# A two-block transformer on one core: first attention beside the later input projections and a split output projection

## What is computed

```
xn   = rmsnorm(x, g)
qa, ka, va, qb, kb, vb, f = split(xn @ w_in)          # widths 512,128,128,512,512,512,8
qa, ka, qb, kb            = rmsnorm per head of 64
out_a = softmax(qa ka' / 8 + alibi, window 128, one sink logit per head) va   # 8 heads, 2 kv heads
c     = cumsum(log_sigmoid(f + b))
out_b = softmax(qb kb' / 8 + c[t] - c[s], causal) vb                          # 8 heads
x = x + concat(out_a, out_b) @ w_out                  # 1024 x 1024
x = x + relu(rmsnorm(x) @ w_up)**2 @ w_down           # width 4096
```

## Time and profile before

| | us |
|---|---|
| median of 3 runs | 1303.53 (1301.13 to 1305.73) |
| profiled execution, its own time | 1305.39 |
| its span, first to last instruction | 1303.6 |
| busy: PE, DVE, ACT, POOL | 1236.2, 681.0, 430.3, 454.6 |
| mean granted TensorE clock | 0.963 |

### The profile page before, as it was taken

How to read it: one execution, slowest core, us unless ns; L and a number is a source line. 1 busy time by engine, 2 the same in 40 slices (tenths; PEclk the granted TensorE clock), 3 DMA queues, 4 the chain that set the end, 5 groups by cost and what they waited for, 6 DMA issues and landing times.

```text
span 1303.6 us, 17163 instructions
## 1 busy us (share of the span) xinstructions
PE 1236.2 (95%) x6252; PEld 1021.3 (78%) x6252; DVE 681.0 (52%) x979; ACT 430.3 (33%) x764; POOL 454.6 (35%) x188
## 2 busy tenths in 40 slices
PE   5899999999898999999989999899999999999997
PEld 4787777789676888888878888777788888888886
DVE  5555356535996875874356621785671131321315
ACT  5444234234312423423333210442442232241331
POOL 3435000044343545354453422210244535344340
PEclk9899669999898999999988999999999999999999
DMA  6323000034453565564333322302233223323211
GB/s 222 114 81 105 25 2 1 1 114 132 151 170 115 193 210 176 184 219 162 128 98 94 94 65 65 90 1 81 65 113 114 88 90 102 108 79 115 81 49 64
DMA packets 71157, 135.65 MB, mean 104 GB/s; under 512 B 6953, under 2 KB 9769, under 8 KB 71081
## 3 DMA queue, kind: packets, MB, share of 16 engines
q1 hardware_dynamic: 53730, 98.46, 24.4%
q10 hardware_dynamic: 17358, 36.27, 8.5%
HBM read 131.80 MB, written 2.13 MB: 103 GB/s over the span
## 4 chain that ended last, share of the span: by engine, by line
PE 64%; DVE 16%; issue 14%; ACT 3%; POOL 2%; DMA 1%; DVEq 0%; ACTq 0%; POOLq 0%
PE gemm L843 20%; PE gemm L844 20%; PE gemm L845 20%; DVE mod_acc L1483 4%; POOL w_lo L439 2%; DVE nmax L1598 1%; PE aux L1207 1%; DVE prob_t L1365 1%; PE aux L891 1%; DVE gemm L1597 1%; DMA wm<-in_w_mod 1%; DVE xt_lo L1273 1%; DVE xr L1267 1%; DVE xr L1262 1%; ACT junk L502 1%
## 5 line engine op out<-in xcount | busy, mean ns | idle before, releaser
L439 POOL TENSOR_TENSOR w_lo<-w_raw,w_hi 128x1024 fp32r<-128x1024 f32 (+1 forms) x180 | 449.4, 2516 | 812.0 <-ACT w_hi L488 408.8
L843 PE MATMUL gemm<-xt_hi,w_hi 128*128 128x512 f32 (+1 forms) x704 | 255.8, 363 | 6.7 <-issue 4.6
L845 PE MATMUL gemm<-xt_hi,w_lo 128*128 128x512 f32 (+1 forms) x704 | 254.7, 362 | 0.0
L844 PE MATMUL gemm<-xt_lo,w_hi 128*128 128x512 f32 (+1 forms) x704 | 254.7, 362 | 0.0
L843 PE MATMUL gemm<-w_hi,ht_hi 128*128 128x512 f32 x512 | 203.0, 396 | 6.4 <-POOL w_lo L439 6.4
L844 PE MATMUL gemm<-w_lo,ht_hi 128*128 128x512 f32 x512 | 202.1, 395 | 0.0
L845 PE MATMUL gemm<-w_hi,ht_lo 128*128 128x512 f32 x512 | 201.9, 394 | 0.0
L625 ACT ACTIVATE w_hi<-w_raw 128x1024 fp32r<-128x1024 f32 x124 | 125.5, 1050 | 207.5 <-PE gemm L845 127.3
L843 PEld LDWEIGHTS gemm<-xt_hi,w_hi 128*128 128x128 f32 x704 | 133.9, 190 | 28.6 <-issue 5.9
L845 PEld LDWEIGHTS gemm<-xt_hi,w_lo 128*128 128x128 f32 x704 | 133.8, 190 | 20.1
L844 PEld LDWEIGHTS gemm<-xt_lo,w_hi 128*128 128x128 f32 x704 | 133.9, 190 | 20.0
(11 more groups left out here) (190 smaller groups left out, 1405.4 us busy)
## 6 DMA issues: line engine op xcount, KB each, us to landing
wm<-in_w_mod ACTq DMA_DIRECT2D x48, 512.0 KB, 4.5
w_raw<-in_w_in SPq DMA_DIRECT2D x32, 512.0 KB, 3.8
w_raw<-in_w_up SPq DMA_DIRECT2D x32, 512.0 KB, 3.8
w_raw<-in_w_down SPq DMA_DIRECT2D x32, 512.0 KB, 3.6
w_raw<-in_w_mlp_in SPq DMA_DIRECT2D x32, 512.0 KB, 4.1
w_raw<-in_w_mlp_out SPq DMA_DIRECT2D x32, 512.0 KB, 3.6
w_raw<-in_w_out SPq DMA_DIRECT2D x16, 512.0 KB, 3.6
x<-in_x SPq DMA_DIRECT2D x4, 512.0 KB, 7.8
```

The source lines that it names most:

```text
L439: pool.tensor_tensor(w_lo[s % 2][:, ks, 0:width], raw[q][:, :, 0:width], w_hi[s % 2][:, ks, 0:width].bitcast(F32), ALU.subtract).then_inc( ...
L843: pe.matmul(bank, lh, rh, start=(k == 0), stop=False)
L844: pe.matmul(bank, lh, rl, start=False, stop=False)
L845: mm = pe.matmul(bank, ll, rh, start=False, stop=(k == KT - 1))
```

## The change

**Order of the work.** PE, ACT and DVE now run one loop of 70 half steps (`HALVES1`) from tile 8 to the last output half. The 64 units are 32 pairs p of two heads, first all of kind a (p = 0 to 15, query tile by query tile), then all of kind b. An even half step 2p has the scores of pair p and the transposes of pair p - 1, the odd one after it the values of pair p - 1. Three slices of an input tile's depth (nine matmuls) follow in each of the half steps 0 to 31 (`part_product`), which makes tiles 8 to 19.

**Output.** The projection is cut by weight rows: half `kind` takes the four depth slices of out_a or out_b. It makes sixteen products of 12 matmuls (`out_half`), each added to x. Table `OUT1_HALF` places them: for kind a at half steps 34, 36, 38, 40, 42, 44, 47, 49, for kind b at 45, 46, 53, 54, 61, 66, 67, 68. `MIX_TURN` places the turns of the mixed heads, `SPLIT1` ACT's weight splits. The norms and turns of row tiles 0 and 1 stand in half steps 49 to 61, those of tiles 2 and 3 in the MLP's first products.

**Banks.** Scores use `gp[0]` and `gp[1]` alone, tiles from 8 on `gp[2]`, `gp[3]` and `aux[2]`, output halves `gp[2]` and `gp[3]`. The probabilities of a pair of kind a are transposed into one bank, `aux[0]`, those of kind b into `aux[0]` and `aux[1]`; values go to `aux[1]` (kind a) and `aux[2]` (kind b), all other turns to `aux[3]`. `qsq` has one buffer in place of two. The gates' temporaries shrink to three rows and are reused.

```diff
+PAIRS1 = [(kind, n, 2 * j) for kind in range(2) for n in range(TT) for j in range(NH // 2)]
+HALVES1 = 70
+SPLIT1 = {h: (s, q) for s, h0 in ((3, 0), (4, 11), (5, 22), (6, 32), (7, 51)) for q, h in enumerate(range(h0, h0 + 4))}
-            for j in range(N_OUT):
-                slab(SLAB_OUT1 + j, t["w_out"], j * NC, NC)
+            for half in range(2):
+                for q in range(UQ):
+                    src = rows(t["w_out"], half * NC, q % 2)[:, :, (q // 2) * NC:(q // 2 + 1) * NC]
+                    unit(q, src, NC, 4 * (SLAB_OUT1 + half - 1) + q + 1)
...
+            def turn_probs(p):
+                kind, n, h = PAIRS1[p]
+                blocks = score_blocks(n, kind)
+                pe.wait_ge(exp_done, 2 * p + 2)
...
+            def values(p):
+                kind, n, h = PAIRS1[p]
+                blocks = score_blocks(n, kind)
+                pe.wait_ge(turn_read, turned_before(p) + kind + 1)
...
+            def out_half(kind, n, j):
+                e = OUT1_ORDER.index((kind, n, j))
...
+                for k in range(4):
+                    lh, ll = lhs(4 * kind + k)
+                    rh, rl = w_hi[w][:, 4 * j + k, :], w_lo[w][:, 4 * j + k, :]
...
+            for h in range(HALVES1):
+                p = h // 2
+                if h % 2 == 0:
+                    if p < len(PAIRS1):
+                        scores(p)
+                    if 1 <= p <= len(PAIRS1):
+                        turn_probs(p - 1)
+                elif 1 <= p <= len(PAIRS1):
+                    values(p - 1)
+                for g in range(PHASE, 16):
+                    if tile_end(g) + 3 == h:
+                        turn_heads(g)
+                if h == 3:
+                    forget_turns()
+                for g, k0, k1 in tile_groups(h):
+                    part_product(g, k0, k1)
...
+                for kind, n, j in halves_of(OUT1_HALF, h):
+                    out_half(kind, n, j)
```

More of the change, by code:

```diff
@@ L594, in _ @@
-            turn = TURN1
-            for i, step in enumerate(STEPS1):
-                if i < len(U1):
-                    n, kind, h = U1[i]
-                    exp_unit(i, score_cols(n, kind), i % 16)
-                for what, k in step:
-                    if what == "M":
-                        for half in range(2):
-                            w = turn[("M", k, half)]
-                            act.wait_ge(turned, w + 1)
-                            did(act.activation(xt_hi[:, 4 * half:4 * half + 4, k * P:(k + 1) * P],
-                                               aux[w % 2][:].rearrange("p (k s) -> p k s", k=4), ACT.Copy), turn_hi)
@@ L607, in _ @@
[L607 to L616 removed]
+                    did(act.activation(c_parts[0:NH, :], frow[0:NH, 2, :], ACT.Copy), c_hi_done)
@@ new lines, in _ @@
+                if h in NORM2_TURN:
+                    m, half = NORM2_TURN[h]
+                    xt_high(NT_2 + m, m, halves=[half])
+                for kind, n in halves_of(MIX_TURN, h):
+                    mix_high(kind, n)
+                if h == 33:
+                    load(gain2[:], spread(t["mlp_norm_g"]), gain2_loaded)
+                if h in SPLIT1:
+                    high_of(*SPLIT1[h])
+            norm2_squares(3)
+            first_root(STAT_N2 + 3)
+            xt_high(NT_2 + 2, 2)
@@ new lines, in mix_turns @@
+            def mix_turns(kind, n):
+                e = MIX_ORDER.index((kind, n))
+                pe.wait_ge(heads_out, TT * kind + n + 1)
+                if e == 0:
+                    pe.wait_ge(qk_stored, 16)
+                else:
+                    pe.wait_ge(mix_read, e)
+                if kind == 1 and n >= 2:
+                    pe.wait_ge(xt_lo_done, 2 * (NT_2 + n - 1))
+                src = mixed_a[:, n, :] if kind == 0 else mixed_b[:]
+                for j in range(4):
+                    mm = pe.transpose(aux[3][:, j * P:(j + 1) * P], src[:, j * P:(j + 1) * P], ident[:])
+                mm.then_inc(mix_turned, 1)
@@ L1320, in _, with head_rows @@
                     hms_done)
+            def head_rows(g):
+                s, m = g // 4, g % 4
+                heads = 2 if s == 1 else NH
+                bank = banks[in_bank(g)]
                 dve.wait_ge(hrs0_done, g + 1)
```

596 lines of the change are left out of this document (367 added, 229 removed).

## The result

The changed kernel takes 1306.85 us (median of 20 runs, 1303.66 to 1311.0), the kernel before on the same chip 1305.82 (20 runs, 1290.34 to 1316.41). The ratio is 1.0043, with a 95% interval of 1.0022 to 1.0064: slower by 0.4%, where 0.9% faster was forecast. It is not the quotient of these medians, because every ratio here leaves out the runs over 1.5% above the fastest of the same kernel as slow ones, which are eight of the twenty before and none of the change. The profiled execution of the change took 1308.12 us around a span of 1306.3, with a mean granted clock of 0.971 (before 1305.39, 1303.6 and 0.963).

A forecast was written before the change was run, and what follows sets the result against it. PE, busy 95% of the span, bounds the kernel; the stretch loses clock and waits. Work 199.2 + 3 + 14.1 + 0.9 + 5 = 222.2 against 233.9 us, so 1303.5 - 11.7 = 1292 us; range 1283 to 1304.

The forecast's parts named there:

- clock in the stretch: Half steps 55 to 60 and 62 to 65: new waits lower the granted clock to 0.81 over 21.6 us, costing 5 us.
- gates: Half steps 4 to 9: the gates' DVE work delays maxima and copies PE needs, 3 us, bounds 0 and 6.
- banks: Only two score banks: PE waits for DVE's copies in eight half steps from 48 to 64, with 32 14.1 us.
- work at 2.4 GHz: Second attention's queries to first MLP product: products, transposes and both head kinds that stay, 199.2 us of 233.9.
- the slow rival: Clock falls at half step 48 and stays low until 66: 36 us in place of 5, 1323 us, chance 0.10.
- wrong if the low clock comes back for over 15 us: Sign against the forecast, which expected mean granted clock over the stretch to rise from 0.91 to about 0.97.
- The old waits: Old stretch from the second attention's queries to the MLP: 12.1 us lost to waits, all forecast to go.
- the old loss: Old stretch loses 34.7 us, 22.6 to the clock and 12.1 to waits, all forecast to go.
- the 6 us of the forecast's mark: First 32 half steps: the forecast is wrong if PE's waits there add up to over 6 us.
- the forecast's mark of 3 us: From the MLP's start to the end: forecast unchanged, and wrong if that time changes by over 3 us.
- DVE's pacing of the first half: Rival: DVE and ACT make each of 32 half steps 0.4 us longer, 12.8 us, giving 1304 us, chance 0.13.
- weight slab: Rival: slabs 3 and 4, split between exponentials, come late; two waits of 5 us give 1302 us, chance 0.05.

The follow-up runs named there:

- Experiment 2: The change with six dummy products between transposes and values in eight half steps from 48 to 64 where PE waits: 1302.31 us, ratio 1.0017 to the kernel before.
- experiment 5: The change with the sixteen output halves dealt out evenly, norm turns and first MLP slab splits moved with them: 1290.54 us, ratio 0.9915 to the kernel before.
- experiment 4: The change with the MLP's turns of norm rows 2 and 3 one product earlier: 1302.06 us, ratio 1.0005 to the kernel before.
- Experiment 3: The change with all 18 products of a pair in the even half step and none in the odd one: 1305.56 us, ratio 1.0027 to the kernel before.
- experiment 1: The kernel before with 48 dummy products of 512 columns ahead of the scores of the first two query tiles: 1303.01 us, ratio 0.9972.
- experiment 6: The change with slab 3's four splits moved from half steps 0 to 3 to 4, 5, 7, 9: 1307.23 us, ratio 1.0029 to the kernel before.
- experiment 8: The change with the first two modulation weight loads issued at half step 60 of the attention: 1307.49 us, ratio 1.0034 to the kernel before.
- Experiment 9: The change with slab 3's splits at half steps 4, 5, 7, 9 and the gates eight half steps later and spread: 1304.47 us, ratio 1.0024 to the kernel before.
- experiment 7: The change with output halves dealt out evenly, slab 3's splits later and the MLP's row turns one product earlier: 1289.16 us, ratio 0.9895 to the kernel before.
- experiment 10: The change with output halves dealt out evenly, slab 3's splits moved, and the gates later and spread: 1288.23 us, ratio 0.9867 to the kernel before.
- experiment 11: Experiment 10 with the MLP's row turns one product earlier and two modulation loads at half step 60: 1283.78 us, ratio 0.9828 to the kernel before.

## Why the prediction was wrong

The forecast was 1292 us; its own sum for the profiled stretch was 222.2 us, the profile has 232.4. Term by term:

| term | forecast, us | profile of the change, us |
|---|---|---|
| clock in the stretch | 5 | 12.1 |
| waits (gates 3, banks 14.1, last heads 0.9) | 18.0 | 15.8, PE's idle time |
| work at 2.4 GHz | 199.2 | 204.5, what is left |
| stretch | 222.2 | 232.4 |
| from the first MLP product to the end, against before | 0 | +3.8 |

The clock's 12.1 us come from the stage table: 0.02 of 108.89 and 0.08 of 123.49 us. With the table's rounding they are good to 1 us.

**The clock in the new waits was the step that failed.** The price of 5 us came from stretches of the first MLP and was applied to 21.6 us of work. These stretches were a poor likeness: they hold four waits of 2.00, 3.61, 2.84 and 5.32 us, two of them for POOL and not for DVE, with products of 512 columns around them, where the change has eight waits of 0.85 to 1.78 us among transposes and value products of 64 columns. That this is why the price came out low is argued, not tested. The runs showed 12.1 us in its place, 9.9 of them behind half step 32. In the change the low clock did not end with the waits: from 279 on it stayed through the values and transposes of the last two pairs (0.50 in 280 to 290) and into the output halves, whose first products behind 290.4 still took 0.63 us instead of 0.39. Experiment 2 shows the cost by filling the waits, experiment 5 by taking them away. The size is that of one profile; the same code in experiment 4 lost about 7 us (0.97 over 228.74 us). The bounds, 0 and the 36 us of the slow rival, did hold it. The range reached only to 1304, because the forecast took the low end and gave everything above to a rival with a chance of 0.10. The outcome lies between the two. Its mark, "wrong if the low clock comes back for over 15 us", was passed: the stage table gives 24.1 us at 1.2 GHz.

**The old waits were counted too high.** The forecast took what its work and clock left of the old stretch, 12.1 us, for waits, and let all of them go. PE was idle for only 8.4 us there, by the earlier trace rows. The other 3.7 us were work that the rows used for the sum do not show, and work does not go with the waits. In the change the work exceeds 199.2 by 5.3 us; how much of that the old kernel had too is not separated. Some of it can be seen in the first half: pairs of two blocks without a turn followed each other at 143.26 and 149.80, 6.54 us; the forecast's rows give 2.22 + 18 x 0.227 = 6.31. An edge where products begin or end costs time that rows within a run do not show; if all of the difference is that, it comes to 3.7 us over 16 pairs. Experiment 3 got 0.10 us a pair back by halving the edges, which fits.

**Removing the old loss was right.** The long stretch of low clock is gone, and experiment 1 shows that it was worth at least 15.2 us. POOL's wait before the MLP went as forecast.

**The waits were right in place and nearly in sum, and mistaken in weight.** Eight places and 11.1 us, where 13.6 were forecast. But the sum already said that the change puts 18 us of waits in place of 12, and measured it is 15.8 in place of 8.4. All of the forecast gain was clock. The kernel before, on the three chips of the experiments, follows a line in its mean granted clock: 9.9 us less per 0.01 more, and 1301.4 to 1302.1 us at 0.970. The change's 20 runs lie on a line of 9.7 us per 0.01, with 1309.5 at 0.970. At equal clock the change is thus 7 to 8 us slower. The two lines come from different chips, but experiments 6 and 8, which gained nothing and ran on one of the three, lie at 1309.1 and 1308.1. The mean clock of all runs of the change is 0.972 where the kernel before has 0.963 to 0.966 on the three chips, which gives 6 to 9 us back.

**The gates were right in size by luck.** Three us were forecast for them and 3.7 measured in front of kind a's values. But 2.8 of these end before the gates begin (experiment 6): their cause is POOL's subtractions, which the forecast passed over because POOL "was idle through the whole old attention". Moving them beside DVE's operations is what the term missed. The gates' own wait, at 99.24, is 0.45 us. The first half has 3.3 us of idle time, under the 6 us of the forecast's mark, and about 2 us of clock behind it; it took 108.9 us instead of about 104. Experiment 9, with both gone, measured 104.2.

**The MLP was not the same.** "The MLP behind is the same, and starts in the same state" was false: the norms of row tiles 2 and 3 now run in its first products, and ACT reaches the first modulation loads 2.8 us later. In the two profiles 3.8 us appear, over the forecast's mark of 3 us. They are not clock, which is higher in the change (0.97 for 0.96 up to block 2): PE is idle for 3.3 us more there. Experiments 5, 7 and 1, and 10 against 11, put it at some 3 us; experiments 3 and 4 do not show it.

**The rivals.** The clock did fall behind half step 48, as the slow rival had it, but with some 10 us and not 36, and not throughout: it was up again from 266 to 279. DVE's pacing of the first half showed as one late pair, not as 0.4 us a step. No weight slab came late.

What stays open: why the granted clock falls at one wait and not at another of the same length, and why the same code lost 12 us to it in one profile and 7 in another.

## What to carry to other kernels

When an interleaving moves filler work beside a latency chain, deal the filler out to every place where the chain is waited for. The same sixteen output halves made this kernel 0.4% slower in one order and 0.9% faster in another. Count waits put in against waits taken out before any gain in clock; if the sum is positive, the change lives on the clock alone, and the runs of both kernels should be compared at equal clock. Count the old waits from PE's idle time and not as what a sum of work leaves over. And check what an engine off the path now runs beside: POOL's pass, on nobody's path itself, held up DVE here.

## What was not expected of the hardware

- A DVE operation of 0.17 us took 1.68 and 2.30 us while POOL subtracted in SBUF, and ended with POOL's instruction. The scan of 8x512 took 2.66 us beside POOL and 1.21 without. The kernel before has it too: an operation on 128x2 elements took 1.68 us at 57.23, beside POOL (54.17 to 58.89), and PE waited 1.87 us at 60.01 for what follows it.
- The low clock stayed when PE was busy again: at 280 to 290 us it was 0.50 while PE was busy for 8.31 of 10 us.
- The time of one kernel follows its mean granted clock closely from run to run: 1290.32 us at 0.983 and 1305.30 at 0.963 for the old kernel on the same chip.
